# S5 chunk outputs by transposes, three sums on strips of the array, and a z block ahead of the state-space loop

## The reference

```python
proj = hn @ w_in                                   # z, xbc, dt, u5, gate_a, gate_b
xbc_c, new_conv = causal_depthwise_conv(xbc, conv_buf, conv_w, conv_b)
dt = softplus(dt_raw + ssd_dt_bias)                # 16 heads
y_ssd, new_ssd = ssd_chunked_scan(xh, dt, a, b, c, ssd_h0)
y_ssd = rms_norm((y_ssd + ssd_d * xh) * silu(z), ssd_norm_g)
branch_a = y_ssd @ w_ssd_branch
y_s5, new_re, new_im = s5_scan(u5, ...)            # complex diagonal state, 64 groups of 16 channels
glu = y_s5 @ w_glu + b_glu
merged = sigmoid(gate_a) * branch_a + sigmoid(gate_b) * glu_part
h = x + merged @ w_mix_out
h = h + memory_attention(rms_norm(h), ...)         # 4 heads, 256 memory tokens
h = h + hier_moe(rms_norm(h), ...)                 # routers: 4 groups, 8 experts each, top 2
```

## Time and profile before

| | |
|---|---|
| median of 3 runs | 1143.79 us (1143.48 to 1144.6) |
| profiled execution | 1144.06 us, span 1141.9 us |
| TensorE busy | 993.6 us (87%) |
| weight loads (PEld) busy | 666.6 us (58%) |
| VectorE busy | 460.7 us (40%) |
| ScalarE busy | 304.6 us (27%) |
| POOL busy | 52.7 us (5%) |
| mean granted TensorE clock | 0.944 |
| moved by DMA | 297.68 MB |

### The profile page before, as it was taken

How to read it: one execution, slowest core, us unless ns; L and a number is a source line. 1 busy time by engine, 2 the same in 40 slices (tenths; PEclk the granted TensorE clock), 3 DMA queues, 4 the chain that set the end, 5 groups by cost and what they waited for, 6 DMA issues and landing times.

```text
span 1141.9 us, 15982 instructions
## 1 busy us (share of the span) xinstructions
PE 993.6 (87%) x6675; PEld 666.6 (58%) x6675; DVE 460.7 (40%) x787; ACT 304.6 (27%) x609; POOL 52.7 (5%) x76
## 2 busy tenths in 40 slices
PE   6999999998999999999898999977677778776564
PEld 4787567985778999999866964423231323231121
DVE  5989956304567644565555330120202020201014
ACT  4142124225437425545334341100000000000002
POOL 1603200001010000000000000000000000000000
PEclk9999999999999999999999999988887978887888
DMA  9492424003535374542588858999999999999994
GB/s 269 116 234 81 158 100 143 6 38 90 169 109 203 129 295 148 193 149 74 198 295 310 321 222 331 421 421 420 421 421 422 422 422 421 420 421 422 422 416 152
DMA packets 92434, 297.68 MB, mean 261 GB/s; under 512 B 21053, under 2 KB 31001, under 8 KB 68172
## 3 DMA queue, kind: packets, MB, share of 16 engines
q1 hardware_dynamic: 89812, 288.81, 66.3%
q0 software_dynamic: 2112, 7.28, 1.9%
q10 hardware_dynamic: 440, 0.59, 0.2%
HBM read 286.76 MB, written 9.90 MB: 260 GB/s over the span
## 4 chain that ended last, share of the span: by engine, by line
PE 36%; SPq 32%; DVE 3%; DMA 2%; issue 2%; ACT 1%; DVEq 0%; ACTq 0%
SPq L624 30%; PE bank L1649 5%; PE bank L1650 5%; PE bank L1651 5%; PE bank L1280 3%; PE bank L1929 2%; PE bank L1978 2%; PE bank L1660 2%; PE bank L1662 2%; PE bank L1661 2%; PE bank L1575 2%; SPq L622 1%; PE bank L1620 1%; DMA ring<-in_state_ssd_dram 1%; DMA work<-in_w_exp_down_dram 1%
## 5 line engine op out<-in xcount | busy, mean ns | idle before, releaser
L1929 PE MATMUL bank<-ring,work 128*32 128x512 f32 x704 | 130.9, 680 | 37.2 <-DMA ring<-in_w_exp_gate_dram 19.4
L1295 PE MATMUL bank<-work,ring 128*128 128x320 f32 (+1 forms) x480 | 125.6, 419 | 0.0
L1649 PE MATMUL bank<-ops,usplit 128*128 128x320 f32 x368 | 114.1, 310 | 1.1 <-DVE usplit L2384 1.1
L1650 PE MATMUL bank<-ops,usplit 128*128 128x320 f32 x368 | 113.9, 310 | 0.0
L1651 PE MATMUL bank<-ops,usplit 128*128 128x320 f32 x368 | 113.9, 309 | 0.0
L1945 PE MATMUL bank<-ring,work 128*32 128x512 f32 x352 | 74.2, 818 | 40.7 <-DMA ring<-in_w_exp_down_dram 30.0
L1295 PEld LDWEIGHTS bank<-work,ring 128*128 128x128 f32 x480 | 90.1, 190 | 30.8 <-issue 1.0
L2384 DVE TENSOR_TENSOR usplit<-ring,usplit 128x2048 fp32r<-128x2048 f32 x32 | 73.3, 2291 | 62.3 <-ACT usplit L994 62.3
L1929 PE MATMUL bank<-work 128*32 128x512 f32 x256 | 85.7, 689 | 14.1 <-DMA work<-in_w_exp_up_dram 6.8
L1929 PEld LDWEIGHTS bank<-ring,work 128*32 128x32 f32 x704 | 32.0, 123 | 100.0 <-issue 80.3
L994 ACT ACTIVATE usplit<-ring 128x2048 fp32r<-128x2048 f32 x32 | 61.4, 1919 | 51.9 <-PE bank L1651 36.7
(11 more groups left out here) (451 smaller groups left out, 1587.1 us busy)
## 6 DMA issues: line engine op xcount, KB each, us to landing
ring<-in_w_exp_up_dram SPq DMA_DIRECT2D x45, 1024.0 KB, 26.0
ring<-in_w_exp_gate_dram SPq DMA_DIRECT2D x43, 1024.0 KB, 26.0
ring<-in_w_exp_down_dram SPq DMA_DIRECT2D x43, 1024.0 KB, 26.4
ring<-in_w_in_dram SPq DMA_DIRECT2D x11, 2048.0 KB, 9.2
work<-in_w_exp_gate_dram SPq DMA_DIRECT2D x16, 1024.0 KB, 22.4
work<-in_w_exp_up_dram SPq DMA_DIRECT2D x16, 1024.0 KB, 26.4
work<-in_w_exp_down_dram SPq DMA_DIRECT2D x14, 1024.0 KB, 26.0
ring<-in_w_glu_dram SPq DMA_DIRECT2D x4, 2048.0 KB, 8.1
```

The source lines that it names most:

```text
L1295: ins = nc.tensor.matmul(b[:, 0:N], wv[:, k, P * (m % 4):P * (m % 4 + 1)], src[:, k, 0:N], start=(k == 0), stop=(k == KT - 1))
L1649: nc.tensor.matmul(b[:, 0:T], wh, hi_[:, k], start=(k == 0), stop=False)
L1650: nc.tensor.matmul(b[:, 0:T], wh, lo_[:, k], start=False, stop=False)
L1929: ins = nc.tensor.matmul(psum[part][ES * x:ES * (x + 1), :], xs[i % 2][:, kk, x], wt[x][:, k], start=(kk == 0), stop=(kk == KT - 1))
```

## The change

- **S5.** `chunk_sum` closes fy after the eight tap products; the chunk outputs are turned by eight transposes into a bank of their own (job ty), and VectorE adds them to `u5T` (`chunk_outputs`) after ScalarE's copy of fy. The second taps (kk1) come after the first step. VectorE's order is six `block_taps`, then an addition, taps 6, an addition, taps 7, and the other additions.
- **Strips.** dtT: `wdt` is widened to 32 columns (16 of zeros), k goes to strip k mod 4 of 32 columns, and dt3 sums and turns the four by products with `fold4`. The norm's sum: the same with 32 columns of ones (job ss4), copied by ScalarE, summed by one product with ones a ga block later (ssy), the scale divided by 32. Logits: strips of 64 columns for even and odd k, folded by `fold2`. POOL makes the two fold matrices and clears `wdt` among its constants; SyncE waits for the constants before it loads `wdt`.
- **z block 3** is done ahead of the loop, two products after each slice c and two after the second decays; the loop has three z products to a round for blocks 4 to 6. ScalarE copies block 3 before the first states, blocks 4 and 5 in rounds 3 and 6.
- **Split 4** on VectorE moves from behind the eight normalising operations to behind the fourth.

```diff
-    j += ["ye0", "yo0", "ye1", "yo1", "kk0", "kk1"]
+    j += ["ye0", "yo0", "ye1", "yo1", "kk0"]
     for ft in range(KT):
-        j.append(f"fy{ft}")
+        j += [f"fy{ft}", f"ty{ft}"]
         if ft + 2 < KT:
             j += [f"ye{ft + 2}", f"yo{ft + 2}"]
+        if ft == 0:
+            j.append("kk1")
...
-    j += [f"ga{m}" for m in range(4)] + ["ssy"]
-    j += [f"ga{m}" for m in range(4, KT)] + [f"gb{m}" for m in range(4)]
+    j += [f"ga{m}" for m in range(4)] + ["ss4", "ga4", "ssy"]
+    j += [f"ga{m}" for m in range(5, KT)] + [f"gb{m}" for m in range(4)]
...
-        wdt = of_early(KT, HEADS)
+        wdt = of_early(KT, 2 * HEADS)
...
             load_block(BIDX["mk0"])
+            sp.wait_ge(s["consts"], 1)
...
+            q(pool.tensor_copy(fold4[:, :], ident[:, 0:HEADS]))
+            for i in range(1, 4):
+                q(pool.tensor_tensor(fold4[:, :], fold4[:, :], ident[:, 32 * i:32 * i + HEADS], ALU.add))
+            q(pool.tensor_tensor(fold2[:, :], ident[:, 0:NG + NG * NE], ident[:, 64:64 + NG + NG * NE], ALU.add))
+            pool.memset(wdt.rearrange("p k n -> p (k n)"), 0.0)
...
             decay(0)
             decay(1)
+            rest_z(3)
...
-                if t and t % 2 == 0:
-                    rest_z(t // 2 + 2)
+                if t in (3, 6):
+                    rest_z(t // 3 + 3)
...
                 if m == 4:
 
+                    got(act, "ss4")
+                    emptied(act.activation(yr1, bank("ss4")[:, 0:T], ACT.Copy), "ss4")
+                if m == 5:
                     done(act, "ssy")
                     act.activation(yr0, yv, ACT.Sqrt).then_inc(s["yr"], 1)
...
-                        ins = nc.tensor.matmul(b[0:HEADS, 0:T], wdt[:, k], hnT[:, k], start=(k == 0), stop=(k == KT - 1))
+                        r0 = 32 * (k % 4)
+                        ins = nc.tensor.matmul(b[r0:r0 + 32, 0:T], wdt[:, k], hnT[:, k], start=(k < 4), stop=(k >= 4))
...
-                        ins = tr(b[0:R, HEADS * c:HEADS * (c + 1)], dtS[0:HEADS, P * c:P * c + R], HEADS)
+                        ins = nc.tensor.matmul(b[0:R, HEADS * c:HEADS * (c + 1)], dtS[:, P * c:P * c + R], fold4[:, :], start=True, stop=True)
...
                 for d in range(Q):
-                    nc.tensor.matmul(b[:, NCK * d:T], kbd[ft // 4][:, ft % 4, Q - 1 - d], u5T[:, 0:Q - d, ft],
-                                     start=(d == 0), stop=False)
+                    ins = nc.tensor.matmul(b[:, NCK * d:T], kbd[ft // 4][:, ft % 4, Q - 1 - d], u5T[:, 0:Q - d, ft],
+                                     start=(d == 0), stop=(d == Q - 1))
+                    if d == Q - 1:
+                        end(ins, f"fy{ft}")
+                b = take(f"ty{ft}")
                 done(pe, f"ye{ft}")
                 done(pe, f"yo{ft}")
                 for i in range(Q):
-                    ins = nc.tensor.matmul(b[:, NCK * i:NCK * (i + 1)], yT[ft % 2][0:NCK, Q - 1 - i].rearrange("p s h k -> p (s h k)"),
-                                           ident[0:NCK, 0:NCK],
-                                           start=False, stop=(i == Q - 1))
-                end(ins, f"fy{ft}")
+                    ins = tr(b[:, NCK * i:NCK * (i + 1)], yT[ft % 2][0:NCK, Q - 1 - i].rearrange("p s h k -> p (s h k)"), NCK)
+                end(ins, f"ty{ft}")
...
             taps(0)
-            taps(1)
             for ft in range(KT):
                 chunk_sum(ft)
                 if ft + 2 < KT:
                     chunk_out(ft + 2)
+                if ft == 0:
+                    taps(1)
...
                 end(ins, f"cb{c}")
+                rest_z(2 * c, 2 * c + 2)
...
             decays(0)
             decays(1)
+            rest_z(6, KT)
...
-                    rest_z(4 * t, 4 * t + 1)
+                    rest_z(KT + 3 * t, KT + 3 * t + 1)
                     if t < KT - 1:
                         old_states(t + 1)
-                    rest_z(4 * t + 1, 4 * t + 2)
+                    rest_z(KT + 3 * t + 1, KT + 3 * t + 2)
...
                     for k in range(NB):
-                        if k == 4:
-                            rest_z(4 * t + 2, 4 * t + 3)
...
-                    rest_z(4 * t + 3, 4 * t + 4)
+                    rest_z(KT + 3 * t + 2, KT + 3 * t + 3)
...
-                    b = take("ssy")
+                    b = take("ss4")
                     pe.wait_ge(s["ysq"], KT)
                     for k in range(KT):
-                        ins = nc.tensor.matmul(b[:, 0:T], ones[:, :], ysq[:, k], start=(k == 0), stop=(k == KT - 1))
-                    end(ins, "ssy")
+                        r0 = 32 * (k % 4)
+                        ins = nc.tensor.matmul(b[r0:r0 + 32, 0:T], ones[:, 0:32], ysq[:, k], start=(k < 4), stop=(k >= 4))
+                    end(ins, "ss4")
+                if m == 5:
+                    b = take("ssy")
+                    done(pe, "ss4")
+                    end(nc.tensor.matmul(b[:, 0:T], ones[:, :], yr1, start=True, stop=True), "ssy")
...
-                ins = nc.tensor.matmul(psum[6][0:NG + NG * NE, 0:T], wr[:, k], tT[k], start=(k == 0), stop=(k == KT - 1))
+                r0 = 64 * (k % 2)
+                ins = nc.tensor.matmul(psum[6][r0:r0 + NG + NG * NE, 0:T], wr[:, k], tT[k], start=(k < 2), stop=(k >= KT - 2))
...
+            def chunk_outputs(ft):
+                done(dve, f"fy{ft}")
+                got(dve, f"ty{ft}")
+                v = u5T[:, :, ft]
+                emptied(TT(v, v, bank(f"ty{ft}")[:, 0:T].rearrange("p (j c) -> p j c", j=Q), ALU.add), f"ty{ft}")
+
+            for ft in range(6):
+                block_taps(ft)
             for ft in range(KT):
-                block_taps(ft)
+                chunk_outputs(ft)
+                if ft + 6 < KT:
+                    block_taps(ft + 6)
...
-            split_unit(4)
+                if m == 3:
+                    split_unit(4)
```

More of the change, by code:

```diff
@@ L282, in layer @@
         sel16 = sb("sel16", [P, 4, 2])
-        early = sb("early", [P, 2092])
+        fold4 = sb("fold4", [P, HEADS])
+        fold2 = sb("fold2", [P, NG + NG * NE])
+        early = sb("early", [P, 2220])
         early_at = [0]
@@ L556, in _ @@
             load_block(BIDX["mk0"])
-            small(wdt[:, :, :], a["w_in"][0][:, COL["dt"]:COL["dt"] + HEADS].rearrange("(k p) n -> p k n", p=P), "ld_small")
+            sp.wait_ge(s["consts"], 1)
+            small(wdt[:, :, 0:HEADS], a["w_in"][0][:, COL["dt"]:COL["dt"] + HEADS].rearrange("(k p) n -> p k n", p=P), "ld_small")
             small(wr[:, :, 0:NG], a["w_router_group"][0].rearrange("(k p) n -> p k n", p=P), "ld_small")
@@ L573, in _ @@
                 load_block(n)
-            got(sp, "fy7")
+            got(sp, "ty7")
             done(sp, "s5o1")
@@ L888, in _ @@
                     got(act, "dtT")
-                    emptied(act.activation(dtS[0:HEADS], bank("dtT")[0:HEADS, 0:T], ACT.Copy), "dtT")
+                    emptied(act.activation(dtS, bank("dtT")[:, 0:T], ACT.Copy), "dtT")
                 if m == 8:
@@ L964, in decay, with rest_z @@
                     act.activation(dm[hd % 8], dm[hd % 8], ACT.Exp, scale=-1.0).then_inc(s["csm"], 1)
+            def rest_z(m):
+                act.wait_ge(s["zf"], m - 2)
+                act.activation(zT[:, m], psum[6 + (m - 3) % 2][:, 0:T], ACT.Copy).then_inc(s["ze"], 1)
             decay(0)
             decay(1)
+            rest_z(3)
             for g in range(2):
@@ L1045, in _ @@
                 if m == 4:
-                    done(act, "fy7")
+                    done(act, "ty7")
                     act.activation(u5_hi, u5T, ACT.Copy).then_inc(s["u5_hi"], 1)
@@ L1538, in _, with rest_z @@
                         end(ins, f"ecs{i}")
+            def rest_z(n0, n1):
+                for n in range(n0, n1):
+                    m, k = 3 + n // KT, n % KT
+                    if k == 0:
+                        have(f"z{m // 4}")
+                        if m >= 5:
+                            pe.wait_ge(s["ze"], m - 4)
+                    ins = nc.tensor.matmul(psum[6 + (m - 3) % 2][:, 0:T], blk(f"z{m // 4}")[:, k, P * (m % 4):P * (m % 4 + 1)],
+                                           hnT[:, k], start=(k == 0), stop=(k == KT - 1))
+                    if k == KT - 1:
+                        ins.then_inc(s["zf"], 1)
             pe.wait_ge(s["xc"], CT)
@@ L1565, in _ @@
             decays(1)
-            def rest_z(n0, n1):
-                for n in range(n0, n1):
-                    m, k = 3 + n // KT, n % KT
-                    if k == 0:
-                        have(f"z{m // 4}")
-                        if m >= 5:
-                            pe.wait_ge(s["ze"], m - 4)
-                    ins = nc.tensor.matmul(psum[6 + (m - 3) % 2][:, 0:T], blk(f"z{m // 4}")[:, k, P * (m % 4):P * (m % 4 + 1)],
-                                           hnT[:, k], start=(k == 0), stop=(k == KT - 1))
-                    if k == KT - 1:
-                        ins.then_inc(s["zf"], 1)
+            rest_z(6, KT)
```

(5 more changed lines are left out.)

7 lines of the change are left out of this document (2 added, 5 removed).

## The result

The changed kernel took 1129.98 us (median of four executions, 1127.23 to 1132.8), beside 1144.0 for the kernel before on the same chip (1143.48 to 1144.6): a ratio of 0.9878, 95% interval 0.9867 to 0.9889. The forecast was 1123.5, the range 1121.0 to 1128.0. The sign was right; the time lies 2 us above the range and 6.5 above the forecast.

What follows compares the result with a forecast made beforehand. TensorE's path before about 690 us was taken as the bound, the expert weights' stream ending the kernel after it. Terms -8.5, -2.8, -5.4, -2.4 and -1.2 gave -20.3, so 1123.5 us, range 1121.0 to 1128.0.

Steps and rivals of the forecast that it cites:

- Part 3: Fourth z block moved ahead of the state-space loop: products -5.0, entry +0.9, state wait -1.24, in all -5.4 us.
- if the clock falls in or after the S5 stage: One of the signs listed as showing the forecast wrong, beside additions holding banks and late weight splits; no size given.
- rival C: TensorE's new gap ahead of the state-space loop lowers the clock, costing 1.7 us on the path: 1125.2; chance 0.14.
- Part 1: S5 chunk outputs: eight transposes replace 16 identity products, a step 5.22 us, second taps moved: -8.5 us.
- Part 2: dt products on four strips of 32 columns in 1.2 us, turned by fold4 products: -2.8 us.
- Part 4: The norm's sum on strips plus one product instead of sixteen instructions, with a split moved: -2.4 us.
- Part 5: Logits in pairs on two strips of 64, three of four pairs gaining 0.5, turn +0.3: -1.2 us.
- rival A: S5's new transposes go at the pace of wide ones, 0.113 us each: 1126; chance 0.14.
- The bank wait at ye3: In S5, TensorE waits for VectorE's first addition to free the bank that ye3 takes: +0.5 us.
- rival B: Strips in dt, norm and logits overlap only by half, as program order would have it: 1126.7; chance 0.08.
- Nothing: New POOL operations at the start and SyncE's new wait cost nothing; TensorE's first transpose waits for x until 7.92 us.
- Rivals D and E: D: expert weight stream was the bound anyway, 1143.5, chance 0.02. E: clock at 1.2 GHz through S5, 1152, chance 0.01.

Runs made afterwards that it cites:

- a1: The changed kernel unchanged, run again with a profile; profiled execution 1133.93 us, six executions with median 1134.74 us, ratio 0.9885.
- a2: The changed kernel unchanged, profiled once more: 1130.61 us.
- a3: The changed kernel unchanged, profiled a further time: 1124.68 us.
- e2: The kernel before with only the z block's move: median 1145.61 us, ratio 1.0017.
- e3: The changed kernel with the old S5 chunk outputs, leaving z move and strips: median 1138.78 us, ratio 0.9946.
- e1: The changed kernel with the z block back in the loop, four products a round: median 1130.84 us, ratio 0.9886.
- e4: The kernel before with only the new S5 part: median 1139.28 us, ratio 0.9943.
- e5: The kernel before with only the three strip products and the moved split: median 1137.74 us, ratio 0.9937.
- g1: The kernel before with the new S5 part and seven unread products in two TensorE waits: median 1136.3 us, ratio 0.9942.
- g2: The kernel before with only seven unread products in two TensorE waits: median 1143.49 us, ratio 0.9993.
- f1: The changed kernel with one z product of each round put amid the narrow ones: medians 1127.38 and 1126.03 us, ratios 0.9851 and 0.9847.
- f3: The changed kernel with a z product amid the narrow ones and seven unread products in two waits: medians 1124.69 and 1125.41 us.
- f2: The changed kernel, order unchanged, with seven unread products in two TensorE waits: median 1133.7 us, ratio 0.9902.

## Why the prediction was wrong

**The step that failed** is in Part 3: "In the state-space loop each round loses one product, the one amid the eight narrow ones", 8 x 0.62 = 5.0, with everything around it at the clock of before. The prediction's own sign of being wrong, "if the clock falls in or after the S5 stage", is what came. The products went, as priced, but the one that I took out was the wide work that broke up a run of narrow ones; without it the granted clock fell in or right behind the loop. In the six profiles of kernels with the moved block and neither remedy (after, a1, a2, a3, e2, e3) the clock fell, 5 us or more after the loop had begun and before ga, in five: at 327.3, 321.5, 303.2, 338.3 and first 296.0 us, each 1.4 to 2.1 us behind the end of a run of narrow products (in a1 1.4, in e2 2.1); in the six with the old loop (before, e1, e4, e5, g1, g2) and in the four with a z product put back amid the narrow ones (f1 and f3, twice each) in none. The one profile of f2 had none either, though its times say that other executions did. The fall is shown; that narrow products without wide ones between them are its cause rests on f1 against the changed kernel and f3 against f2, where only the order differs, and the slow executions of kernels with the old loop (e1, e4, g1, g2) say that it is not the whole of it.

I had looked for a fall where TensorE idles (rival C) and priced "with that gap filled I take the clock as full there" at the entry. The Trainium skill, "TensorE: Matmul & The Clock Gate", Part 1, section "HAM oscillation — how this bites in real kernels", leads the same way: it puts the fall down to waits between bursts of matmuls. The rows at 80 us and at the entry agree with it in part: a fall followed the wait of 2.29 us at 80 us, none followed the 2.32 us of before at the same place, and none the 1.82 us at the entry. Those of the loop do not agree: 43.90 of 43.90 us busy, and then 17.00 of 17.00 at 0.51. The measurement decides: absence of idle time in the rows is no proof that the clock holds. Busy is not the same as much work here: the narrow instructions start 0.107 us apart for 8 columns each (277.07 to 278.78, by 16), those of 320 columns 0.27.

**The size of it.** The profiled execution missed by 4.0 us of the sum. Of these 1.7 us lie behind the loop, and 0.8 us around 80 us (1.55 lost, 0.73 gained ahead of it), which is no part of the change's own places (it is in a2, e1, e4 and f1 too, and not in a1, a3, e2 or e3); the other 1.5 us are terms that were a little too large. The typical execution loses more; a1's had 17 us at 1.2 GHz.

Point by point, by the steps of the prediction, in the profiled execution:

| step | forecast | measured | |
|---|---|---|---|
| Part 1, S5 | -8.5 | -8.1 (48.99 to 40.90) | right |
| Part 2, dt | -2.8 | -2.8 (4.41 to 1.22; turn 0.25 to 0.67) | right |
| Part 3, loop | -6.24 | -5.76 (58.81 to 53.05) | 0.62 was 0.56 a round (5.76 less the wait of 1.24, by 8) |
| Part 3, entry | +0.9 | +0.85 (283.24 - 268.04 to 273.94 - 257.89) | right |
| Part 4, norm, with all up to the first logits | -2.4 | -2.0 (13.36 gained to 15.37) | near: 2.35 gained behind the two sums; 0.26 of it lost around a stretch at 1.2 GHz that both traces have in the attention (570.9 before, 556.0 after) |
| Part 5, logits and the turn | -1.2 | -1.0 (15.37 gained to 16.37) | right: three pairs gained 0.53 each and the fourth nothing, the turn cost 0.5 (0.25 to 0.77) |
| clock at 80 us | 0 | +0.8 (0.73 gained ahead of it, 1.54 lost) | not foreseen |
| clock behind the loop | 0 | +1.7 | the failed step |
| sum | -20.3 | -16.3, and 16.4 by the span | |

- *Part 1.* A step is 5.31 us (227.08 to 232.39) for 5.22; a transpose of 40 columns 0.076 (their 0.61 to the next start, by 8), between my 0.07 and the bound 0.113, so rival A fell. The idle time ahead of the first block product is 1.80. The bank wait at ye3, forecast at 0.5, was 0.2. The forecast told these times by the clock time of before, and all of S5 stands 2.06 us earlier now: VectorE's first addition was done at 209.2 us, just as forecast (211.3 less 2.06), and TensorE came to the bank at 209.1, 0.2 later than forecast (210.9 less 2.06).
- *Part 2 and rival B.* Sixteen instructions of 320 columns on four strips took 1.22 us, 3.5 times as fast as one after the other would be (16 x 0.269). Rival B, and with it the prediction's reckoning from program order, would have had 2.4. The norm's sum has 1.21 plus 0.54 in place of 4.31 by its instructions, and 2.35 of that reached the products behind.
- *Part 3.* No wait for a state is left, and rounds are 6.61 us (280.55 - 273.94), two of them 7.14 and the last, without the next pair's old states, 5.73. Rival C's mechanism, a fall at the new gap ahead of the loop, was real in a1, a2 and a3 (0.50 from 273.7, 0.56 from 272.5 us), not in the first profile. It was the smaller cause.
- *Nothing.* TensorE's first transpose waited for the last constant and not for x, and started at 7.77 us, ahead of the 7.92 of the earlier trace rows.
- *Rivals D and E.* The stream followed TensorE one for one (experts 16.37 earlier, end 16.4), and S5 ran at 1.00 to 240 us.

None of the rivals had a fall in a stretch without waits. The forecast time is about what the kernel takes when its clock holds: f3, with the work of the change and seven products hidden in waits, has 1124.69 and 1125.41 as medians, for 1123.5 forecast. It is also the best version here: 0.9821 and 0.9828 of before, beside 0.9878 and 0.9885 for the change as it stood.

What stays open: which places are slow in the slower executions of e1, e4, g1 and g2, with the old loop, and of f1 and f2; why one execution has a fall and the next has none; and why e5 alone stayed within 0.7 us, when the kernel before itself ran from 1142.75 to 1147.59 beside it.

## What to carry to other kernels

Before wide work is taken out from between narrow products, ask what it does for TensorE's clock: price both the instructions' time and one fall behind the narrow run, and if a remedy is free (another order of the same products) use it at once. Read the granted clock beside busy time, since a stretch can be busy throughout and still at half speed. And a gain of some microseconds should be judged by the spread of executions too: a part that moves the lowest time and widens the spread has found something that a single profile may not show.

## What the runs showed of the hardware

- TensorE's clock falls to 1.2 GHz with the engine busy all the time (43.90 of 43.90 us before, 17.00 of 17.00 at 0.51), 1.4 to 2.1 us behind runs of 16 instructions of 8 columns, in some executions of a program and not in others; times of one program then lie 11 us apart.
- Strips overlap even when two instructions in a row (one f32 product) go to the same one: 16 x 320 columns in 1.22 us, 3.5 times the pace of the earlier trace rows.
- An f32 transpose costs less when it is narrow: 0.076 us at 40 columns, beside about 0.065 at 24 and 0.113 at 128.
